# Undecayed keys of a chunked gated recurrence: one ScalarE instruction in place of two GpSimd instructions

## What is computed

```python
def forget_gate(f_logits, lb):
    f = lb + (1.0 - lb) * jax.nn.sigmoid(f_logits.astype(jnp.float32))
    return split_heads(jnp.log(f)), split_heads(1.0 - f)      # decay in logs, keys

def step(state, xs):                                          # one chunk
    qc, kc, vc, gc = xs
    b = jnp.cumsum(gc, axis=2)
    b_last = b[:, :, -1:, :]
    k_dec = kc * jnp.exp(b_last - b)
    new_state = (jnp.exp(b_last[:, :, 0, :, None]) * state
                 + jnp.einsum('bhck,bhcv->bhkv', k_dec, vc))
    o_inter = jnp.einsum('bhtk,bhkv->bhtv', qc * jnp.exp(b), state)
    ...
    o = o_inter + jnp.einsum('bhts,bhsv->bhtv', scores, vc)
```

## Time and profile before

| | |
|---|---|
| time, median of 3 runs | 2312.58 us (2309.34, 2312.58, 2317.04) |
| span of the profiled execution | 2315.0 us |
| of it before the recurrence | 0 to 552 |
| recurrence (`heads_stage`) | about 552 to 984 |
| output projection, choice, experts | 984 to 2315 |
| PE / DVE / ACT / POOL busy over the span | 94% / 70% / 45% / 22% |

### The profile page before, as it was taken

How to read it: one execution, slowest core, us unless ns; L and a number is a source line. 1 busy time by engine, 2 the same in 40 slices (tenths; PEclk the granted TensorE clock), 3 DMA queues, 4 the chain that set the end, 5 groups by cost and what they waited for, 6 DMA issues and landing times. The chain is left out here.

```text
span 2315.0 us, 38576 instructions
## 1 busy us (share of the span) xinstructions
PE 2187.4 (94%) x14737; PEld 1480.7 (64%) x14885; DVE 1609.4 (70%) x2233; ACT 1041.0 (45%) x1329; POOL 504.9 (22%) x537
## 2 busy tenths in 40 slices
PE   7799999998999999899986999999999999999995
PEld 3444444444878787755534777777777777777773
DVE  2749999785679687865566667666666666666666
ACT  3611011456566666644442444543444444543444
POOL 1710001013657567300012111101111011101111
PEclk9899999999999999899977999999999999999998
DMA  9341002454021111375453776667766766667776
GB/s 345 98 73 37 14 23 87 149 161 124 6 55 50 45 57 24 116 263 165 152 189 137 241 232 230 224 218 227 243 220 211 242 218 240 219 221 233 229 233 266
DMA packets 216931, 377.14 MB, mean 163 GB/s; under 512 B 38147, under 2 KB 79619, under 8 KB 216333
## 3 DMA queue, kind: packets, MB, share of 16 engines
q1 hardware_dynamic: 198702, 317.38, 40.7%
q0 software_dynamic: 16528, 56.47, 9.0%
q10 hardware_dynamic: 1616, 2.16, 0.3%
HBM read 313.44 MB, written 62.54 MB: 162 GB/s over the span
## 5 line engine op out<-in xcount | busy, mean ns | idle before, releaser
L89 PE MATMUL pgu<-xhi,mwhi 128*128 128x256 bf16 x2048 | 558.8, 273 | 0.0
L90 PE MATMUL pgu<-xlo,mwhi 128*128 128x256 bf16 x2048 | 558.7, 273 | 0.0
L91 PE MATMUL pgu<-xhi,mwlo 128*128 128x256 bf16 x2048 | 558.6, 273 | 0.0
L2440 DVE TENSOR_TENSOR mwlo<-mwst,mwhi 128x2048 bf16<-128x2048 f32 x187 | 427.0, 2283 | 0.0
L2337 ACT ACTIVATE mwhi<-mwst 128x2048 bf16<-128x2048 f32 x186 | 350.8, 1902 | 0.1
L2345 ACT ACTIVATE thb<-pgu 128x256 f32<-128x256 f32 x128 | 49.0, 383 | 548.0 <-PE pgu L91 548.0
L676 DVE SCALAR_TENSOR_TENSOR co<-u,taps,co 128x1984 f32<-128x1984 f32 (+22 forms) x120 | 234.1, 1951 | 3.7
L2451 DVE SCALAR_TENSOR_TENSOR thb<-thb,pgu 128x256 f32<-128x256 f32 x128 | 53.8, 421 | 259.0 <-ACT thb L2345 259.0
L2273 POOL TENSOR_TENSOR mpflag<-mpflag 1x1 f32<-1x1 f32 x46 | 37.5, 815 | 846.4 <-DVE ysb L2467 579.4
L89 PEld LDWEIGHTS pgu<-xhi,mwhi 128*128 128x128 bf16 x2048 | 200.5, 98 | 24.6
L90 PEld LDWEIGHTS pgu<-xlo,mwhi 128*128 128x128 bf16 x2048 | 200.6, 98 | 24.5
(11 more groups left out here) (397 smaller groups left out, 4399.2 us busy)
## 6 DMA issues: line engine op xcount, KB each, us to landing
mwst<-in_w_gate SPq DMA_DIRECT2D x32, 2048.0 KB, 9.1
mwst<-in_w_up SPq DMA_DIRECT2D x32, 2048.0 KB, 7.9
mwst<-in_w_down SPq DMA_DIRECT2D x32, 2048.0 KB, 7.9
wst<-in_w_in SPq DMA_DIRECT2D x28, 512.0 KB, 6.1
big<-in_ada_w SPq DMA_DIRECT2D x5, 2048.0 KB, 14.6
s_rows<-row SPq DMA_DIRECT2D x16, 520.0 KB, 5.8
u<-in_ada_w SPq DMA_DIRECT2D x8, 1024.0 KB, 6.1
xt<-in_x SPq DMA_DIRECT2D x16, 512.0 KB, 4.4
```

The source lines that it names most:

```text
L89: nc.tensor.matmul(out, lh, rh, start=(first and k == 0), stop=False)
L90: nc.tensor.matmul(out, lh, rl, start=False, stop=False)
L91: ins = nc.tensor.matmul(out, ll, rh, start=False, stop=(last and k == n - 1))
L2440: nc.vector.tensor_tensor(wlo[:, b, ks], wst[:, b % NS, ks], whi[:, b, ks], ALU.subtract)\
```

## The change

`keep` moves from POOL to ACT. `hpflag` and its semaphore go, the operation becomes one ACTIVATE (Identity) with per-partition scale `-g` and bias `g`, both already in `lh`. In ACT's order it stands behind `exps` of its own unit.

```diff
-                def keep(h, i):
-                    h, i = at(h, i)
-                    p, n, d = i % 2, size(i), UNITS[i][0]
-                    wait(pool, th_ok, U(h, i) + 1)
-                    if i < 2:
-                        wait(pool, hd_ok, h * 6 + 3 * i + 3)
-                    wait(pool, kt_ps, U(h, i - 1))
-                    wait(pool, pf_ok, U(h, i) + 1)
-                    nc.gpsimd.tensor_tensor(pflag[:], pflag[:], pflag[:], ALU.mult).then_inc(pf_ok, 1)
-                    nc.gpsimd.tensor_scalar(KK[:, p, 0:n], G[:, p, 0:n], -1.0, lh[:, d, 2:3], ALU.add, ALU.mult).then_inc(kk_ok, 1)
...
-                keep(0, 0)
-                keep(0, 1)
                 wait(pool, zero_ok, 1)
                 decay_k(0, 0)
...
                         if there(i + 1, prev, cur, nxt):
                             decay_k(h, i + 1)
-                        if there(i + 2, prev, cur, nxt):
-                            keep(h, i + 2)
...
+                def keep(h, i):
+                    h, i = at(h, i)
+                    p, n, d = i % 2, size(i), UNITS[i][0]
+                    wait(act, th_ok, U(h, i) + 1)
+                    if i < 2:
+                        wait(act, hd_ok, h * 6 + 3 * i + 3)
+                    wait(act, kt_ps, U(h, i - 1))
+                    nc.scalar.activation(KK[:, p, 0:n], G[:, p, 0:n], ACT.Identity, bias=lh[:, d, 0:1], scale=lh[:, d, 2:3])\
+                        .then_inc(kk_ok, 1)
...
                 gate(0, 0)
                 logs(0, 0)
                 gate(0, 1)
+                keep(0, 0)
                 exps(0, 0)
                 logs(0, 1)
+                keep(0, 1)
                 turn(0, 0)
...
                         if there(i + 2, prev, cur, nxt):
                             exps(h, i + 2)
+                            keep(h, i + 2)
```

More of the change, by code:

```diff
@@ L933, in heads_stage @@
         flag = m.sb("hflag", [1, 1])
-        pflag = m.sb("hpflag", [1, 1])
         pout = K["pout"]
@@ L942, in heads_stage @@
         at0_ok = m.sem("at0_ok")
-        hd_ok, pf_ok, ng_ok = m.sem("hd_ok"), m.sem("pf_ok"), m.sem("ng_ok")
+        hd_ok, ng_ok = m.sem("hd_ok"), m.sem("ng_ok")
         w_in, w_hi, w_lo = GW_.loaded, GW_.hi_ok, GW_.lo_ok
@@ L1063, in _ @@
                 nc.gpsimd.memset(segm[:], 1.0).then_inc(msk_ok, 1)
-                nc.gpsimd.memset(pflag[:], 0.0).then_inc(pf_ok, 1)
                 wait(pool, msk_ok, 1)
```

## The result

| | changed kernel | kernel before |
|---|---|---|
| time, median (lowest to highest) | 2318.21 us (2312.29 to 2325.97), 19 runs | 2313.28 us (2308.88 to 2319.23), 19 runs |
| ratio, 95% interval | 1.0020 (1.0012 to 1.0028), +4.9 us | |
| profiled execution: span (its own time) | 2323.7 us (2325.70) | 2315.0 us (2317.04) |

So 0.2% slower, which is inside the 0.3% about which one measurement tells nothing, and the interval leaves zero out. The profiled execution of the changed kernel lies 7.5 us above its median, the one of before 4 us.

The account below looks back on a forecast made before the run. PE bounds the recurrence, so only delays at its waits count: 1.5 + 0.8 + 1.7 + 0.3 + 0.5 + 0.4 = 5.2 us slower, added to the median 2312.6 for 2317.8 us; range 2310 to 2325.

Parts of the forecast that it names:

- insertion: ScalarE, between the exponentials and KX: KK now comes behind se, so KX starts later; 10.7 us in the sum.
- relief: VectorE, scan to KX: copy L1315 no longer held by POOL's removed work; 1.0 us a place (0.68 to 1.71), 5.6 summed.
- PE is the bound, ACT's time is free, the ACTIVATE costs 0.80: Recurrence: PE busy 357.5 of 381 us, ACT 247; 24 more do not bind; ACTIVATE taken as 0.81 us.
- the delays of `KX`: POOL's KX waits for KK: 0.86 us later at unit 12, about 1.33 where se waits for the chain of states.
- the start: Recurrence start up to unit 2's scores: two ACTIVATEs in a busy ACT row plus 0.86; +1.5 us (0.9 to 1.9).
- The collision rival: Late GpSimd cross blocks run into VectorE's scan, slowing scan and KX, 1.1 us at seven places: 7.7 more, 2325.5; chance 0.28.
- as POOL time this is worth nothing: POOL at unit 13: the removed 1.10 + 0.68 us lie behind the cross blocks, where POOL then waits for ACT.
- units 9, 12 and 13: PE's waits for cross blocks: unit 9 +0.8 us; 12 and 13 together +0.6, three times, +1.7.
- Unit 27: Scores with the narrowest cover: KX 0.86 us later against 0.38 of cover, +0.5 us.
- units 4 to 8 and 14 to 17 are covered: PE in these units: no waits expected from the later KX; waits there would show the prediction wrong.
- the wait for `S` of 2.81 shrinks and isn't kept: PE ahead of units 19, 29: wait shrinks 1 to 2 us, not kept; unit 29's KX +0.3, unit 19 0.
- unit 39 through `low` to the weights' load: End of stage: POOL's delay at the last unit passes to the output projection; 1.33 - 1.0, +0.4 us.

Follow-up runs that it names:

- ln_pool: Changed kernel with the ACTIVATE moved right behind its unit's Ln, both old GpSimd operations kept into an unread scratch: 2310.43 us, 0.9992 of the kernel before.
- ln_flag: Changed kernel with the ACTIVATE moved right behind its unit's Ln, only the 1x1 GpSimd product kept: 2301.65 us, 0.9953 of the kernel before.
- pool_kept: Changed kernel with both old GpSimd operations still run at their old place, into an unread buffer: 2334.04 us, 1.0096 of the kernel before.
- spare_act: Kernel before plus an ACTIVATE of the same form at the change's place, into an unread buffer: 2311.97 us, 0.9996 of the kernel before.
- behind_ln: Changed kernel with the ACTIVATE moved ahead of B's scan, right behind its unit's Ln: 2302.78 us, 0.9957 of the kernel before.
- again: The changed kernel run once more without an edit: 2319.58 us, 1.0028 of the kernel before.
- before_early_w: Kernel before with the output weights' loads issued ahead of the third head's last store: 2307.83 us, 0.9977 of the kernel before.
- change_early_w: Changed kernel with the output weights' loads issued ahead of the third head's last store: 2311.10 us, 0.9988 of the kernel before.
- ahead_of_se: Changed kernel with the ACTIVATE moved between the exponential of B and the one making se: 2315.35 us, 1.0003 of the kernel before.
- ln_early_w: behind_ln with the output weights' loads issued ahead of the third head's last store: 2297.42 us, 0.9937 of the kernel before.

## Why the prediction came out right, and where its steps did not

The forecast was 2317.8 and the median is 2318.2; the difference was put at +5.2 and measured as +4.9. The sum was right by cancellation of two larger terms, so that its closeness is luck. The runs give these two terms, against the kernel before, in us:

| `KK` made on ACT | POOL's work kept | POOL freed | relief |
|---|---|---|---|
| behind `se` (the change) | +20.8 | +6.3 | 14.5 |
| behind Ln | -1.6 | -10.5 | 8.9 |
| what the place costs | 22.4 | 16.8 | |

(`ln_pool` ran on another chip than the other three; beside `ln_flag` on its own chip its relief is 8.8.) In my sum, insertion was 1.5 + 1.33 + 3 × 1.58 + 1.33 + 0.5 + 1.33 = 10.7 and relief 0.58 + 3 × 1.0 + 1.0 + 1.0 = 5.6. The steps that failed are these two sizes: the insertion was put at 10.7 and measures 16.8 to 22.4, the relief at 5.6 and measures 8.9 to 14.5. The sum also took them as independent. The relief came out at 14.5 at one place and 8.9 at the other; as times this difference of 5.6 is not clear of noise (the runs of `pool_kept` alone spread over 11.6), but the rows above show that at the two places the relief reaches the path in two ways, by the small sums and `S` at the one and by the copy ahead of the exponentials at the other.

**Right: PE is the bound, ACT's time is free, the ACTIVATE costs 0.80.** `spare_act` shows the second by itself.

**Right: the delays of `KX`.** 0.86 and about 1.33 behind the old time were forecast. It begins 0.97 to 0.99 behind the exponential of `B` where no chain is in front, and mostly 1.46 to 1.62 with the chain (2.75 at unit 20), against 0.08 to 0.16 before: 0.9 and 1.4. At unit 12 of the changed kernel:

```profile
674.12 0.63 ACT L1160 ACTIVATE B<-B 128x512 f32<-128x512 f32 x1
674.65 0.24 ACT L1167 ACTIVATE se<-sm 128x60 f32<-128x60 f32 x1
674.79 0.80 ACT L1138 ACTIVATE KK<-G,lh 128x512 f32<-128x512 f32 x1
```

```profile
675.72 1.27 POOL L1080 TENSOR_TENSOR KX<-KK,B 128x512 f32<-128x512 f32 x1 [7.21 <-ACT KK L1138]
...
678.42 3.23 POOL L1087 TENSOR_TENSOR KX<-KX,se 128x128 f32<-128x128 f32 x3
681.61 1.27 POOL L1094 TENSOR_TENSOR of<-of,rsb 128x512 f32<-128x512 f32 x1
```

**Right: the start,** +1.5 forecast and +1.4 measured, from the stage's first product on.

**Wrong in size: the relief at DVE.** It was taken as 1.0 a place, between 0.68 and 1.71. At unit 13 the stretch from the scan's end to the subtraction's end was 2.73 before, 2.41 in the change (0.3 less) and 1.89 in `behind_ln` (0.8 less). Over 40 units it sums to 70.4 before, 65.8 in the change (67.1 in `again`), 48.9 in `behind_ln`. But in `pool_kept`, where POOL's work is not gone, it is 68.7, and the copy's mean is down there too (628 ns, against 967 before and 594 in `again`). So at this place the removal gives this stretch 1.6 to 2.9 us in all, and the copies became short mostly with the place of `KK`, by which POOL's block comes later, and not by the removal. What the removal gave the change shows in the small sums and in the wait for `S`, which the prediction had as a constant.

**The collision rival is real as a mechanism.** I had said that it decides where the cross blocks end more than 0.7 behind the scan's call. At unit 13 of the changed kernel they end at 678.42 + 3.23 = 681.65, and the scan was called at 679.79:

```profile
679.79 1.23 DVE L1304 TENSOR_TENSOR_SCAN B<-segm,E 128x512 f32<-128x512 f32 x1 [0.79 <-ACT E L1149]
681.05 0.63 DVE L1311 COPY sm<-B 128x16 f32<-128x16 f32 x1
681.79 1.64 DVE L1314 TENSOR_TENSOR B<-B,sm 128x512 f32<-128x512 f32 x1
```

1.86 behind the call, and yet the scan takes 1.23 and not the 1.75 of the earlier trace rows. It begins 0.02 ahead of the third cross block, and now it is this one that takes 1.84; before, the third cross block began 0.16 ahead of the scan (671.22) and took 0.83. The changed kernel, then before:

```profile
679.81 1.84 POOL L1087 TENSOR_TENSOR KX<-KX,se 128x384 f32<-128x384 f32 x1
```

```profile
671.06 0.83 POOL L1100 TENSOR_TENSOR KX<-KX,se 128x384 f32<-128x384 f32 x1
```

The collision's victim was not what I had priced (the scan and `KX`). It is the cross blocks themselves, which took 2.23 there and take 3.23, and the subtraction. By form over the whole recurrence, before and after, the third cross block:

```profile
L1100 POOL TENSOR_TENSOR KX<-KX,se 128x384 f32<-128x384 f32 x32 | 34.4, 1076 | 0.0
```

```profile
L1087 POOL TENSOR_TENSOR KX<-KX,se 128x384 f32<-128x384 f32 x32 | 42.9, 1342 | 0.0
```

and DVE's copy and subtraction, before and after:

```profile
L1315 DVE COPY sm<-B 128x16 f32<-128x16 f32 x32 | 31.0, 967 | 1.1
...
L1318 DVE TENSOR_TENSOR B<-B,sm 128x512 f32<-128x512 f32 x32 | 23.6, 738 | 1.1
```

```profile
L1311 DVE COPY sm<-B 128x16 f32<-128x16 f32 x32 | 18.7, 584 | 1.1
...
L1314 DVE TENSOR_TENSOR B<-B,sm 128x512 f32<-128x512 f32 x32 | 34.7, 1086 | 1.1
```

The copies win 12.3 us and the subtraction gives 11.1 back; the third cross blocks lose 8.5. In `behind_ln` the cross block is back at 1076 ns, the subtraction at 708. So being late is paid twice, once as itself and once in what it runs into. How much of it lies on the path was not measured by itself; it is within the 16.8 us that the place costs.

The rows agree with the rule of the Trainium skill (SBUF — State Buffer, Who interferes with whom) that issue order and not an operation's shape decides who blocks: with POOL in front the copy and the subtraction wait (1.64 for 0.69), with DVE in front the cross blocks do (3.23 for 2.23). The prediction's sum had used the lock only in the direction in which DVE waits; its rival priced the other direction, but at `KX` and not at the cross blocks.

**Right as said, and the step behind it wrong: "as POOL time this is worth nothing".** At unit 18 of `pool_kept` POOL stands idle for 2.80 us ahead of `KX`, so that its own time is free there too. But the prediction looked for DVE's stand-still only at the copy L1315, on the way from the scan to `KX`. It saw that `se` waits for the chain of states and took 1.33 as a constant, though POOL's operations, when they come later, hold up the small sums ahead of that very chain. With `KK` behind `se`, `pool_kept` lays 15.3 us more of waits for `S` in front of `KX`.

**Half right: units 9, 12 and 13.** Unit 9 was +0.8 and is +1.4 behind the start. At 12 and 13 PE waits 1.22 longer at one and 0.86 less at the other, together about +0.4 where I had +0.6. Unit 27 was put at +0.5 and waits 0.91.

**Wrong: units 4 to 8 and 14 to 17 are covered.** Unit 17's scores wait 0.91 and unit 7's 0.49. The others do not wait.

**Right: the wait for `S` of 2.81 shrinks and isn't kept.** It is gone, and 1.50 at unit 18 and 1.36 at unit 19 stand in its place.

**Not foreseen: the clock at unit 9.** It costs +4.9 us there in each of the three profiles. The text had said that a clock that falls elsewhere can move the whole by 1.6 a time; this one fall is worth three times that. Counted from 576 to 984 the clock costs 18.8 us in the profile of before and 8.5 in that of `before_early_w`, 25.0 in the first of the change and 13.7 in the other two, 10.3 in `behind_ln`. Two profiles of the same recurrence differ by 10 us in this, so that one profile can't say what the change does to the clock as a whole.

**Right as a path, unsettled in size: unit 39 through `low` to the weights' load.** The loads are issued at 957.41 before; in the change:

```profile
968.42 2.68 SPq L1053 DMA_DIRECT2D hhi<-in_w_out  x4
```

In `again` they are issued at 961.79, 4.4 later than before, where the sum had 0.4. There the late weights also hold up ACT (6.24 us of waiting for their load) and behind it a readout product that PE needs:

```profile
972.43 2.08 PE L1597 MATMUL pj<-sqb,mean_p 128*128 128x512 f32 x2 [4.81 <-ACT sqb L1181]
```

The same wait is 2.16 before, and it does not appear in `before_early_w` and `change_early_w`.

**Where the 18.4 us between `again` and `behind_ln` lie.** From 555 us to the milestone of each:

```profile
555.00:987.65 432.65, 393.14 (x2901) 325.84 (x2947) 311.13 (x678) 311.21 (x443) 220.59 (x202) 0.97 0.19 56
```

```profile
555.00:969.29 414.29, 387.40 (x2900) 324.09 (x2945) 316.81 (x677) 310.22 (x443) 215.48 (x202) 0.98 0.20 59
```

PE is idle for 39.5 us in the one and 26.9 in the other, 12.6 more. The clock costs 3.4 more (13.7 against 10.3). The other 2.3 are not located; ends of matmuls are modelled in the profile, so that short gaps between them read as busy.

**What stays open.** Why the clock falls behind unit 9 in the change. The wait of 1.59 us that goes before it is not enough to explain it: `pool_kept` has the same wait at the same time without a fall, and so has `ahead_of_se` (at 647.47). PE's row in `again`, then in `pool_kept`, and a window behind it in `pool_kept`:

```profile
648.56 0.38 PE L1517 MATMUL pout<-E,KX 128*128 128x32 f32 x2 [1.59 <-issue]
```

```profile
648.55 0.38 PE L1534 MATMUL pout<-E,KX 128*128 128x32 f32 x2 [1.59 <-issue]
```

```profile
652.00:656.00 4.00, 3.95 (x32) 3.72 (x32) 1.27 (x3) 2.79 (x4) 1.01 (x3) 1.00 0.00 0
```

Yet it fell in all four profiles of the changed kernel and its variant with early loads. What else differs there was not found.

## What to carry to other kernels

Moving an operation to an idle engine is two changes: what the old engine is freed from, and where in the new engine's order the result now appears. Price both, and place the instruction at the first point at which its input exists and its engine is not the one being waited for: 0.8 us behind `se` cost 17 us more than behind Ln, and ahead of Ln cost no more than behind it. When a sum of such terms comes out near zero, ask what each term would be alone, since the same change put elsewhere may keep the gain and drop the cost.

## What the runs showed of the hardware that I had not expected

A copy of 16 columns, 0.18 us by itself, averages 952 ns in `ln_pool`, 667 in `ln_flag` and 474 in `behind_ln`. The first two differ by GpSimd's operation of 128x512, which is worth 0.68 us undisturbed and 27.4 us in all in `ln_pool`: its removal takes 9.1 us off DVE's copies. The last two differ by a product of one element, and 6.2 us of the copies go with it. In part DVE pays them elsewhere: the scan averages 1508 ns in `ln_flag` and 1630 in `behind_ln`.

A fall of TensorE's clock costs its 5 us in one piece: behind unit 9 the clock stood at 1.2 GHz from 652 to 660 us, and a stretch of 9.3 us became 14.2. Two kernels that wait the same 1.59 us at the same place need not share the fall.

The runs of before spread over 10 us and those of the change over 14, those of `behind_ln` over 2.1 and of `ln_early_w` over 1.8. There were 19 runs of each of the first two and 5 and 6 of the others, and why their time is steadier was not looked into: PE is still idle for 26.9 us on the way to the milestone in `behind_ln`.
